# Layer 0's input products in three rounded passes, and the running maxima spread head by head

## The reference

```
aq, ak, av, ao (4 heads of 128 each), 16 gate columns, bq (8 heads of 64), bk, bv (2 heads of 64 each)
b      = cumsum(log_sigmoid(f));  dmat = b_t - b_s + i_s  (s <= t);  m_t = running maximum
s      = (aq . ak) * exp(dmat - m_t);   h = (s @ av) / max(|sum s|, exp(-m_t))      # forwards and backwards
window = softmax(rope(norm(bq)) . rope(norm(bk)) with a sink) @ bv
mix    = [sigmoid(ao) * rms_norm(h), window];   x += gate * (mix @ w_out)
```

## Time and profile before

| what | us |
|---|---|
| median of three runs | 1672.75 |
| profiled execution, whole | 1673.68 |
| its span, first to last instruction | 1672.3 |
| start to the first product of the tiles ahead of the heads | 39.8 |
| tiles ahead of the heads, to the start of head 0 | to 64.3 |
| head 0 | 64.3 to 132.5 |
| heads 1, 2, 3 | 55.6, 55.6, 55.9 |
| output product of layer 0 begins | 299.5 |

### The profile page before, as it was taken

The page is one execution under the profiler, slowest core; times in us unless marked ns, Lnnn a source line. Parts: engine busy times, 40 slices in busy tenths (PEclk is TensorE's granted clock), DMA queues, the critical chain, the costliest instruction groups (busy, mean ns, idle before and its releaser), DMA issues.

```text
span 1672.3 us, 25099 instructions
## 1 busy us (share of the span) xinstructions
PE 1572.5 (94%) x9596; PEld 1310.1 (78%) x9596; DVE 1109.3 (66%) x2022; ACT 724.2 (43%) x1349; POOL 476.7 (29%) x385
## 2 busy tenths in 40 slices
PE   6999999989999999989888999989999999999888
PEld 5565566768888888866667999988888888899778
DVE  5467787868777787658767788655454455553764
ACT  2442434353333332344542655544444444454454
POOL 1012104102222100125330111025555555522652
PEclk8999999999999999999999999999999999999999
DMA  9223214415334456502325455554443433444240
GB/s 390 100 101 124 90 64 139 140 37 182 134 138 150 176 191 200 176 29 98 119 78 204 150 187 180 188 166 138 133 131 129 132 133 127 133 139 144 89 144 26
DMA packets 63943, 231.23 MB, mean 138 GB/s; under 512 B 7520, under 2 KB 8544, under 8 KB 63568
## 3 DMA queue, kind: packets, MB, share of 16 engines
q1 hardware_dynamic: 60912, 218.66, 38.4%
q0 software_dynamic: 2192, 6.29, 1.1%
q10 hardware_dynamic: 720, 4.68, 0.7%
HBM read 228.55 MB, written 1.05 MB: 137 GB/s over the span
## 4 chain that ended last, share of the span: by engine, by line
PE 81%; DVE 8%; ACT 5%; issue 3%; DMA 1%; POOL 1%; SPq 0%; ACTq 0%; DVEq 0%; POOLq 0%
PE ps L267 13%; PE ps L269 12%; PE ps L268 12%; PE ps L249 9%; PE ps L1314 4%; PE ps L1315 4%; PE ps L1316 4%; PE ps L257 2%; DVE big L687 2%; PE ps L742 2%; PE ps L732 2%; ACT big L668 2%; PE ps L311 1%; PE ps L635 1%; DMA ring<-in_ada_first 1%
## 5 line engine op out<-in xcount | busy, mean ns | idle before, releaser
L282 DVE TENSOR_TENSOR weights_rest<-ring,weights_rounded 128x1024 fp32r<-128x1024 f32 x192 | 267.9, 1397 | 72.7 <-ACT weights_rounded L276 72.7
L276 ACT ACTIVATE weights_rounded<-ring 128x1024 fp32r<-128x1024 f32 x233 | 244.3, 1053 | 118.3 <-PE ps L1316 94.1
L267 PE MATMUL ps<-h_hi,weights_rounded 128*128 128x512 f32 (+1 forms) x640 | 215.0, 336 | 0.0
L268 PE MATMUL ps<-h_lo,weights_rounded 128*128 128x512 f32 (+1 forms) x640 | 215.0, 336 | 0.0
L269 PE MATMUL ps<-h_hi,weights_rest 128*128 128x512 f32 (+1 forms) x640 | 215.0, 336 | 0.0
L1300 POOL TENSOR_TENSOR big<-scratch 128x512 f32<-128x512 f32 (+1 forms) x44 | 64.2, 1459 | 393.6 <-DVE scratch L1286 393.6
L288 POOL TENSOR_TENSOR weights_rest<-ring,weights_rounded 128x1024 fp32r<-128x1024 f32 x41 | 98.4, 2402 | 177.2 <-ACT weights_rounded L276 177.2
L1240 ACT ACTIVATE scratch<-ps,vectors 128x512 f32<-128x512 f32 (+1 forms) x88 | 59.2, 673 | 192.4 <-PE ps L269 182.2
L249 PE MATMUL ps<-h,ring 128*128 128x512 f32 x288 | 132.1, 615 | 2.2 <-DVE h L488 2.2
L268 PEld LDWEIGHTS ps<-h_lo,weights_rounded 128*128 128x128 f32 x640 | 121.5, 190 | 12.6
L269 PEld LDWEIGHTS ps<-h_hi,weights_rest 128*128 128x128 f32 x640 | 121.5, 190 | 12.5
(11 more groups left out here) (380 smaller groups left out, 3955.5 us busy)
## 6 DMA issues: line engine op xcount, KB each, us to landing
ring<-in_up SPq DMA_DIRECT2D x88, 512.0 KB, 3.8
ring<-in_ada_rest SPq DMA_DIRECT2D x80, 512.0 KB, 4.5
ring<-in_a_in SPq DMA_DIRECT2D x80, 512.0 KB, 3.5
ring<-in_down SPq DMA_DIRECT2D x44, 512.0 KB, 4.2
ring<-in_even SPq DMA_DIRECT2D x20, 512.0 KB, 4.1
ring<-in_ada_first SPq DMA_DIRECT2D x16, 512.0 KB, 9.4
ring<-in_wout SPq DMA_DIRECT2D x16, 512.0 KB, 3.6
ring<-in_odd SPq DMA_DIRECT2D x16, 512.0 KB, 3.5
```

The source lines that it names most:

```text
L267: te.matmul(bank[:, 0:n], wh[:, k, :], hi(k), start=k == 0, stop=False)
L268: te.matmul(bank[:, 0:n], wh[:, k, :], lo(k), start=False, stop=False)
L276: sc.activation(pair[0], place(*key), ACT.Copy).then_inc(*mark("rounded", *key))
L282: ve.tensor_tensor(pair[1], place(*key), pair[0].bitcast(F32), ALU.subtract).then_inc(*mark("rest", *key))
```

## The change

- All 23 tiles of layer 0's input products go through `pe_product3`. Rounding: ScalarE, 23 times. Rests: GpSimd for the values ahead of the heads, for tiles 0, 1 and 4 of every head and tile 2 of head 0; VectorE for the others (tile 3 of every head, tile 2 of heads 1 to 3, gates and keys). A tile's place in the ring is released by its rest.
- h is made as in layer 1: VectorE scales 256 columns (gain and inverse root at once), ScalarE adds the shift and rounds, VectorE makes the rest. All of it stands behind the gains. The rests of gates and keys are put after the first two scalings.
- `pe_pre` runs the three tiles together, one block of 128 input features after another. `act_gates` now waits for the last of them, since the rows that it writes share memory with these tiles' pairs.
- Values (ahead of the heads, and product 3) come out feature by feature; ScalarE copies them, four transposes turn them (`pe_even_turn`), and ScalarE copies them again.
- `MREP` and the ScalarE copies are gone. `pe_spread` makes two matmuls for one head: head 0's after product 2, head i + 1's between the weighing and the transposed heads of head i. The gaps read PSUM.
- In head 0, `pe_gates` moves from behind product 0 to behind product 2.
- At the start, the rows' turning is cut into four parts, ahead of tiles 8, 12, 15 and after the last.

```diff
     def scalar_program():
         act_start()
-        act_modulate(0)
+        act_even_h()
         act_gates()
@@ pe_start
+            if s in (8, 12, 15):
+                pe_rows(s // 4 - 2 + (s == 15))
@@ dve_even_h
+        gains(0, 0, (0, 1), at("mod_added", "first"))
+        ...
+            if x == 1:
+                for t in range(2):
+                    dve_rest(("even_pre", t), PAIR_PRE[t], [])
@@ act_gates
-        sc.wait_ge(*at("product", "even_pre", 0))
+        sc.wait_ge(*at("product", "even_pre", 2))
@@ pool_pre
+        pool_rest(("even_pre", 2), PAIR_PRE[2], [])
+        for s in range(3):
+            pool_even_rest(0, s)
@@ pe_even
-        pe_product(("even", i, 0), BANK[6], TOK, hk(0, TOK))
+        pe_even_product(i, 0, BANK[6])
+        if i == 0:
+            pe_even_turn(("even_pre", 2), VFM0[0], BANK[2])
+        pe_even_product(i, 1, BANK[7])
+        ...
+        pe_even_product(i, 2, BANK[7])
         if i == 0:
             pe_gates()
             te.wait_ge(*at("consts_in", "rest"))
+            te.wait_ge(*at("v_copied", 0))
             pe_spread(0)
@@ pe_even, after the window scores
+        pe_even_turn(("even", i, 3), VFM0[1], BANK[6])
+        pe_even_product(i, 4, BANK[7])
@@ pe_even, after pe_weigh
+        if i + 1 < AH:
+            pe_spread(i + 1)
@@ act_even
+        act_even_round(i, 3)
         sc.wait_ge(*at("product", "even", i, 2))
         sc.activation(ak, BANK[7], ACT.Copy, scale=AD ** -0.5).then_inc(*mark("ak_copied", i))
+        act_even_round(i, 4)
+        if i == 0:
+            act_floors()
+            gap_exps()
         sc.wait_ge(*at("product", "even", i, 3))
+        sc.wait_ge(*at("normed", "even", i, 0))
+        sc.activation(VFM0[1], BANK[6], ACT.Copy).then_inc(*mark("copied", "even", i, 3))
+        act_even_round(i + 1, 0)
+        sc.wait_ge(*at("turned", "even", i, 3))
         sc.activation(av3[:, :, 0:128], v3(BANK[6], 128), ACT.Copy).then_inc(*mark("av_copied", i))
         act_exps(us)
+        act_even_round(i + 1, 1)
@@ dve_even
-            ve.tensor_scalar(W, MREP[:, (dr * AH + i) * TOK + lo:(dr * AH + i) * TOK + lo + n], GT[:, c:c + 1], 0.0,
+            ve.tensor_scalar(W, BANK[SPREAD[dr]][:, lo:lo + n], GT[:, c:c + 1], 0.0,
+        dve_even_rest(i, 2)
         dve_ada(6 * i)
         ...
+        dve_even_rest(i, 3)
         dve_ada(6 * i + 2)
@@ pool_even, after the rope
+        pool_even_rest(i, 4)
+        pool_even_rest(i + 1, 0)
+        pool_even_rest(i + 1, 1)
```

More of the change, by code:

```diff
@@ L404, in pe_start, with pe_rows @@
             ins.then_inc(*mark("product", "ada_first", s))
[L405 to L410, removed]
+        pe_rows(3).then_inc(*mark("rows_turned"))
+    def pe_rows(g):
+        te.wait_ge(*at("rows_copied", g))
+        for j in range(4 * g, 4 * g + 4):
+            ins = te.matmul(BANK[2][:, 2 * j:2 * j + 2], rows2[:, 128 * j:128 * j + 128], v(V_SUM, 2), start=True, stop=True)
+        return ins
     def dve_start():
@@ L472, in pool_modulate @@
[L472 to L489, removed]
@@ new lines, in dve_even_rest, with pool_even_rest, pe_even_product @@
+    def dve_even_rest(i, s):
+        if not even_on_pool(i, s):
+            dve_rest(even_tile(i, s), even_pair(i, s), even_free(i, s))
+    def pool_even_rest(i, s):
+        if even_on_pool(i, s):
+            pool_rest(even_tile(i, s), even_pair(i, s), even_free(i, s))
+    def pe_even_product(i, s, bank):
+        pe_product3(("even", i, s), even_pair(i, s), bank, TOK, even_hi, even_lo, even_rest(i, s))
+    PAIR_PRE = [(rounded(f"pre_rounded_{x}", "big", 5120 + 2 * D * x, D), rounded(f"pre_rest_{x}", "big", 5120 + 2 * D * x + D, D))
+                for x in range(3)]
@@ L499, in build, with pe_even_turn, pe_spread @@
     gate_names = ("if", "ff", "ib", "fb")
-    def pe_pre():
[L502 to L505, removed]
-        pe_norm(KEY0, t1, BANK[1], TOK)
[L508 to L517, removed]
+    VFM0 = (SCR[:, 7332:7844], t1)
+    def pe_even_turn(key, vfm, bank):
+        te.wait_ge(*at("copied", *key))
+        for t in range(4):
+            ins = te.transpose(bank[:, 128 * t:128 * t + 128], vfm[:, 128 * t:128 * t + 128], ident)
+        ins.then_inc(*mark("turned", *key))
+    PRE_BANKS = [3, 0, 2]
+    def pe_pre():
+        for x in range(3):
+            te.wait_ge(*at("rest_pool" if x == 2 else "rest", "even_pre", x))
+        for k in range(KD):
+            te.wait_ge(*at("h_rest", "even", k, 1))
+            for x in range(3):
+                wh, wl = (v3(w, 128)[:, k, :] for w in PAIR_PRE[x])
+                bank = BANK[PRE_BANKS[x]]
+                if x == 2 and k == 0:
+                    te.wait_ge(*at("mod_added", "first"))
+                te.matmul(bank, wh, even_hi(k), start=k == 0, stop=False)
+                te.matmul(bank, wh, even_lo(k), start=False, stop=False)
+                ins = te.matmul(bank, wl, even_hi(k), start=False, stop=k == KD - 1)
+                if k == KD - 1:
+                    ins.then_inc(*mark("product", "even_pre", x))
+        pe_norm(KEY0, t1, BANK[1], TOK)
+    SPREAD = (2, 4)
+    def pe_spread(i):
+        for dr in range(2):
+            te.wait_ge(*at("maxima", dr))
+            te.matmul(BANK[SPREAD[dr]], CT[0:4, C_SEL + 128 * i:C_SEL + 128 * i + 128], rows[6 + dr], start=True,
+                      stop=True).then_inc(*mark("maxima_spread", dr, i))
     def pe_gates():
@@ L1027, in wout_free, with wout_pair @@
     def wout_free(b):
-        return [at("product", "wout", 0, b - PAIRS)] if b >= PAIRS else []
+        return [at("product", "wout", 0, b - PAIRS)] if b >= PAIRS else even_free(AH, b)
+    def wout_pair(b):
+        return even_pair(AH, b)
     def mix_parts(k):
```

141 lines of the change are left out of this document (77 added, 64 removed).

## The result

The changed kernel takes 1694.1 us (median of 4 runs, 1691.4 to 1695.3), the kernel before 1673.3 on the same chip (1670.6 to 1673.9): ratio 1.0131, 95% interval 1.0119 to 1.0144, slower by 21 us. The forecast was 1693.9 us, in a range of 1680 to 1704. The profiled execution spans 1693.4 us, against 1672.3.

What follows compares the result with a forecast made beforehand. TensorE sets each head's front, ScalarE and VectorE increasingly its tail; the shorter front uses up VectorE's slack. Terms 14.8 + 2.5 + 2.5 + 1.3 = 21.1 on 1673.68 give 1694.8, median 0.9 lower: 1693.9 us, range 1680 to 1704.

Steps and rivals of the forecast that it cites:

- Turning rows: At the start: turning the rows in four parts gains 0.5 us (bounds 0 and 3.8), gains ready at 37.6.
- first product: Ahead of the heads: TensorE's first product starts at 45.1 us, against 39.81 before.
- GpSimd cost VectorE: Before the first product: GpSimd's first rest gets in behind VectorE's own two and costs up to 2.5 us.
- First wait: Ahead of head 0's keys' norm: TensorE stands still 11.7 us, until 75.2, for ScalarE's gates and keys' square.
- Second wait: In head 0, ahead of the next rope: TensorE waits 9.7 us for VectorE's norm, ending at 108.5.
- The gaps read from PSUM: VectorE's nine gaps per head: 3.33 us, bounds 2.6 and 4, against 2.58 from SBUF.
- Tile 4's transfer ... just fit: Head 0: the transfer is late and its rounding precedes the gap exponentials, but decays end near 119.5 and just fit.
- the front of heads 1 and 2: From head start to window scores: VectorE's work and GpSimd's rests sum to 30.3 us; TensorE's own front is 26.0.
- Tail: From window scores' start to head end: 27.8 us; head 0 ends at 147.3 against 132.46, 14.8 us later.
- Heads 1 to 3: Periods of 58.1 us in heads 1 and 2 (+2.5 each) and 57.2 in head 3 (+1.3).
- the term for the rests: GpSimd's rests hold VectorE up in each head: 2.5 us beside an `ada` tile, 1.8 at the heads' first VectorE instruction.
- clock falls in every head: Rival: after TensorE's 4 us wait ahead of window scores, heads 1 to 3 lose 2.2 us each: 1700.5; chance 0.14.

Runs made afterwards that it cites:

- b_rows: Kernel before, with only the sums' rows turned in parts between the sums: 0.9996 of the kernel before (0.9987 to 1.0005).
- x_square: Changed kernel; ScalarE squares the keys and copies the values ahead of the gate rows' instructions: 1.0151 of the kernel before.
- x_norm: Changed kernel; in head 0 VectorE scales the norm's queries ahead of conditioning tiles 0 and 1: 1.0147 of the kernel before.
- x_warm: Changed kernel; TensorE gets unread products ahead of the window scores (heads 1 to 3) and behind the numerators (heads 0 to 2): 1.0132 of the kernel before.
- x_lock: Changed kernel; fifth tile's rest moved from GpSimd to VectorE, next head's second tile rounded behind the denominators: 1.0082 of the kernel before.
- c_all: Changed kernel; start and head 0 reordered, spread behind the numerators, fifth tile's rest on VectorE, second tile's rounding behind the denominators: 1665.7 us, 0.9958 of the kernel before.
- x_spread: Changed kernel; TensorE's spread for the next head moved right behind the numerators: 1.0079 of the kernel before.
- x_warm2: x_warm with head 0's two long TensorE waits also filled, by 48 and 40 unread products: 1.0127 of the kernel before.

## Why the prediction was right

**Turning rows and first product.** The gains were ready at 36.5, 1.6 us and not 0.5 earlier; alone (b_rows) the part is worth at most 2.2 us (0.9987), and the runs can't tell it from none. The two rests of the pre tiles took 4.50 us for 2.45, so GpSimd cost VectorE 2.05 where 2.5 stood. First product 43.7 for 45.1. The sum was 1.4 us too late, inside its bounds.

**First wait.** 11.70 for 11.7, and by the cause named: ScalarE's gates from 62.11, then its conditioning rows, then the keys' square at 73.12. x_square removed it through that order.

**Second wait.** 10.02 for 9.7. (The terms as written add up to 108.15 and not 108.5, which makes 9.4 of the 9.7; in the same way those of the front of heads 1 and 2 add up to 30.0 and not 30.3.) The gaps read from PSUM took 3.88 for 3.33 (bounds 2.6 to 4). "Tile 4's transfer ... just fit" was true and weighed more than the sentence did: it is why x_norm gained nothing. The prediction priced waits as they stood, and a learner should note that behind each of the two in head 0, 21.7 us together, stood a second chain. Without the first, the window scores start 4.0 us earlier and not 11.7 (x_square); with the second 4.8 us shorter, 0.6 earlier (x_norm).

**Tail and head 1.** From window scores to head 1's first product 27.0 for 27.8; start 146.4 for 147.3.

**Heads 1 to 3.** First products at 146.42, 204.77 and 265.91 and the output product at 322.84 give periods (first product to first product) of 58.4, 61.1 and 56.9 for 58.1, 58.1 and 57.2. In heads 1 and 2 the window scores start 29.6 and 31.2 us behind that product (forecast 30.3) and the tail takes 28.7 and 30.0 (forecast 27.8), with half clock in both. How long a head is without it, x_warm shows, whose trace has none from 114 to 258 us and no other engine's work changed: head 1 takes 56.6 us there (146.61 to 203.24), its window scores starting 29.6 us behind its first product and its tail taking 27.0. So the prediction's sum for a head was 1.5 us too long, about half of it in the front and half in the tail, and in the changed kernel the clock, which the sum left out, made up for that. VectorE is busy from head start to the maxima without a gap but one of 1.2 us, as the prediction had it, and x_lock shows the term for the rests: 2.07 us of a conditioning instruction and 1.72 of a denominator step, where the prediction had 2.5 at the first place and 1.8 at the second. The page of the Trainium skill it used, "SBUF — State Buffer", section "Who interferes with whom", has VectorE's two-input instructions contend with GpSimd's reads; c_all's 1.11 us for 0.14 agree.

**What was off.** The rival "clock falls in every head" was set aside because the clock is 1.00 in the heads of the kernel before. It did fall, behind the wait ahead of the window scores in each of heads 1 to 3, and these scores take 4.33, 5.49 and 4.38 us where they take 2.85 at full clock, 5.7 us in all (the rival had 2.2 a head). From head 1's first product to the output product the changed kernel takes 9.4 us more than the kernel before; the forecast had 6.3, and x_warm, with most of the half clock gone, has 3.1. So the right sum for these heads is in part two errors that meet: terms that were too long (1.5 us in head 1) and a clock that was priced at nothing. Head 2 shows it least evened out, 3 us over, with 5.49 us for its scores at 0.50 and its first seven products at half clock.

Up to the output product the sum was +21.1 and is +23.6. The missing 2.5 us came back behind it with no change of work: half clock from 330 us on is 38 us in the kernel before and 33 in the changed one, which is 2.7 us of TensorE's time. Such a difference is the scatter of single executions and no effect that these runs show: those of the unchanged kernel before differ by 5 us among themselves, the slower ones at the lower mean clock (1668.9 us at 0.988, 1673.7 at 0.983). The total agreed so closely in part by luck, in the heads and behind them.

## What to carry to other kernels

Rounding a weight into parts moves work from TensorE to the engines that prepare the parts; compare the second busiest engine's load per stage with the stage's length first (VectorE here: 43 of 55.6 us before, 51 of 58.4 after). A wait in the trace is worth its length only if no second chain ends as late: ask what the same instruction would wait for next, and for a moved conditioning or weight step ask which ring place it frees and what the in-order transfers behind it feed. Small waits of TensorE inside a busy stage are worth filling with work it has to do anyway.

## What the runs showed of the hardware

TensorE's waits of 3.05 us ahead of the window scores were followed by half clock (1.2 GHz) in all three heads of the changed kernel; after the same waits, 3.03 to 3.07 us, the scores took 2.85 us at full clock in head 1 of x_square and in heads 2 and 3 of x_spread. After waits of 2.1 us they took 4.26 to 4.55 us in the three heads of c_all, and 2.85 in heads 2 and 3 of x_lock. So the length of this one wait does not say whether the clock falls. Products nobody reads held the clock over the filled stretch (no half clock between 60 and 110 us in x_warm2, 25 us in the changed kernel) and not beyond it (142 to 148 us).

GpSimd's rest is itself held up by VectorE's two-input instructions: 3.37 us at 166.93, where 2.35 is its time elsewhere and the prediction took it to keep its length. VectorE's decays, which read one input from PSUM, ran from 173.73 in their usual 3.34 us beside the rest of 174.65 to 177.00.
